# Adding two product pairs of a seven-product block in PSUM, with one product of each block issued behind the first of the next

## What is computed

```
def hybrid_mixer(xn, ...):
    z = xn @ w_in                                   # 7 x 1024 columns: u, v, b_gate, c_gate, x_in, r_a, r_b
    u, v = gelu(u), layer_norm(gelu(v))
    y_a = (u * chunk_spatial_mix(v, w_s, b_s)) @ w_a_out
    y_b = (b_gate * short_conv(c_gate * x_in)) @ w_b_out
    return (sigmoid(r_a) * y_a + sigmoid(r_b) * y_b) @ w_o

x = x + rms_norm(hybrid_mixer(rms_norm(x)))
x = x + rms_norm((silu(xf @ w_gate) * (xf @ w_up)) @ w_down)      # xf = rms_norm(x), hidden width 2816
```

## Time and profile before

| | us |
|---|---|
| three timed runs | 1603.54, 1603.16, 1603.20 |
| their median | 1603.2 |
| span of the profiled execution | 1601.0 |
| TensorE busy | 1590.6 (99%) |
| VectorE busy | 1081.9 (68%) |
| ScalarE busy | 559.8 (35%) |
| GpSimd busy | 703.9 (44%) |

### The profile page before, as it was taken

How to read it: one execution, slowest core, us unless ns; L and a number is a source line. 1 busy time by engine, 2 the same in 40 slices (tenths; PEclk the granted TensorE clock), 3 DMA queues, 4 the chain that set the end, 5 groups by cost and what they waited for, 6 DMA issues and landing times.

```text
span 1601.0 us, 30253 instructions
## 1 busy us (share of the span) xinstructions
PE 1590.6 (99%) x12427; PEld 1542.2 (96%) x12427; DVE 1081.9 (68%) x1463; ACT 559.8 (35%) x852; POOL 703.9 (44%) x512
## 2 busy tenths in 40 slices
PE   9999999999999999999999999999999999999998
PEld 6889999999999999999978999999999999999997
DVE  8757857797793338868965666766666666575766
ACT  4222332222223336333434532333332233352544
POOL 1011534544544444644730324544444443545375
PEclk9999999999999999999999999999999999999999
DMA  6202011431423333474423313533333345472723
GB/s 216 79 1 80 27 54 34 126 96 44 126 82 110 109 106 121 149 242 133 148 91 120 131 41 110 155 105 100 106 104 104 105 124 178 153 239 80 238 107 133
DMA packets 155283, 184.38 MB, mean 115 GB/s; under 512 B 7355, under 2 KB 138035, under 8 KB 155147
## 3 DMA queue, kind: packets, MB, share of 16 engines
q1 hardware_dynamic: 154987, 182.41, 35.7%
q10 hardware_dynamic: 160, 0.04, 0.0%
HBM read 133.74 MB, written 48.72 MB: 114 GB/s over the span
## 4 chain that ended last, share of the span: by engine, by line
PE 95%; DVE 1%; DMA 1%; POOL 1%; issue 1%; SPq 0%; ACT 0%; DVEq 0%; ACTq 0%; POOLq 0%
PE ps L414 91%; PE ps L449 1%; PE ps L526 1%; DMA pre_gain<-in_mix_pre_g 1%; DVE tp L2213 1%; PE ps L669 0%; PE ps L653 0%; PE ps L424 0%; DMA tp_f<-hid_dram 0%; SPq L783 0%; DVE s_bc L2232 0%; POOL ring_lo L1108 0%; POOL ring_lo L1095 0%; PE ps L503 0%; DVE g L2234 0%
## 5 line engine op out<-in xcount | busy, mean ns | idle before, releaser
L414 PE MATMUL ps<-tp,ring_hi 128*128 128x258 f32 x7292 | 1182.9, 283 | 0.5 <-issue 0.3
L414 PEld LDWEIGHTS ps<-tp,ring_hi 128*128 128x128 f32 x7292 | 1010.6, 190 | 0.9 <-issue 0.5
L414 PE MATMUL ps<-tp,ring_lo 128*128 128x258 f32 x3646 | 744.8, 283 | 0.0
L414 PEld LDWEIGHTS ps<-tp,ring_lo 128*128 128x128 f32 x3646 | 571.3, 190 | 0.0
L1095 POOL TENSOR_TENSOR ring_lo<-ring_f,ring_hi 128x512 fp32r<-128x512 f32 (+1 forms) x228 | 328.3, 1460 | 365.1 <-DVE ring_f L1840 212.5
L1095 POOL TENSOR_TENSOR ring_lo<-stage,ring_hi 128x512 fp32r<-128x512 f32 (+1 forms) x199 | 304.7, 1540 | 400.3 <-ACT ring_hi L1240 399.6
L1240 ACT ACTIVATE ring_hi<-ring_f 128x512 fp32r<-128x512 f32 (+1 forms) x228 | 142.6, 627 | 519.9 <-DVE ring_f L1835 196.2
L1240 ACT ACTIVATE ring_hi<-stage 128x512 fp32r<-128x512 f32 (+1 forms) x199 | 122.0, 617 | 121.1 <-PE ps L414 63.5
L1832 DVE TENSOR_TENSOR ring_f<-stage 128x512 f32<-128x512 f32 (+1 forms) x57 | 46.8, 821 | 135.2 <-PE ps L414 82.7
L1853 DVE TENSOR_TENSOR s_a<-ps,s_a 128x516 f32<-128x516 f32 (+1 forms) x58 | 39.8, 686 | 51.9 <-PE ps L414 51.4
L414 PE MATMUL ps<-tp 128*128 128x512 f32 (+1 forms) x384 | 72.0, 340 | 0.0
(11 more groups left out here) (243 smaller groups left out, 1453.9 us busy)
## 6 DMA issues: line engine op xcount, KB each, us to landing
stage<-in_w_in SPq DMA_DIRECT2D x24, 1024.0 KB, 5.9
ht_dram<-ht SPq DMA_DIRECT2D x44, 258.0 KB, 4.2
hid_dram<-hq SPq DMA_DIRECT2D x40, 258.0 KB, 3.1
stage<-in_w_gate SPq DMA_DIRECT2D x10, 1024.0 KB, 6.6
stage<-in_w_up SPq DMA_DIRECT2D x10, 1024.0 KB, 5.3
tp_f<-hid_dram SPq DMA_DIRECT2D x16, 516.0 KB, 5.5
tp_f<-ht_dram SPq DMA_DIRECT2D x16, 516.0 KB, 8.7
stage<-in_w_down SPq DMA_DIRECT2D x8, 1024.0 KB, 7.1
```

What stands on the lines that cost most here:

```text
L414: ins = pe.matmul(o, w, xc, start=first and n == 0, stop=last and n == 2)
```

## The change

- `PBANK` is another one: products 0 and 2 both land in Y, 4 and 6 both in X. Products 2 and 6 don't clear their pair, so Y then holds P0 + P2, and X holds P4 + P6.
- c11 = P0 + P2 is not made by DVE any more: its consumer reads it in PSUM (`c11_act` on ACT; a product or `gather` on DVE). u1 and u2 become one operation, `u2` = P3 + s1; `u4` = P1 + u2; c22 = P4 + u4, c12 = P5 + u4, c21 = (P4 + P6) + u2. DVE has two operations fewer in each of the 58 runs. Seven runs whose c11 had been put straight to its place have an ACT copy for it.
- The waits of TensorE are now: product 2 for s1 (P0 must be copied before P2 is added to it), 5 for u2, 6 for c22, all of the same run; of the run before, product 0 waits for the reader of c11 (Y), 1 for u4 (W), 3 for c12 (Z), 4 for c21 (X). The first half of a plain run (Z) waits for c12.
- Where a run and its next both have seven products (`piped`), the order is 1, 2, 3, 4, 5 of r, then 0 of r+1, then 6 of r, then 1 of r+1. Before plain runs and at run 2 it is not so.
- The buffers `s_a` and `s_b` take turns as the place of s1 and u2, so s1 of a run doesn't wait for c21 of the run before.

```diff
-PBANK = [Z, W, Y, X, Z, Y, X]
+PBANK = [Y, W, Y, Z, X, Z, X]
...
+def piped(run):
+    return 2 < run < len(RUNS) - 1 and RUNS[run][0] not in QORDER and RUNS[run + 1][0] not in QORDER
+ORDER = []
+for r, (b, _) in enumerate(RUNS):
+    seq = [(r, i) for i in range(1 if piped(r - 1) else 0, 4 if b in QORDER else 7)]
+    if piped(r):
+        seq.insert(-1, (r + 1, 0))
+    ORDER += seq
...
-                    pe.wait_ge({Z: u2_done, W: c22_done, Y: c12_done, X: c21_done}[pair], SIDX[r])
+                    pe.wait_ge(*(c11_read(r) if pair == Y else ({W: u4_done, Z: c12_done, X: c21_done}[pair], SIDX[r])))
             def product(r, p):
+                if p == 6 and piped(r):
+                    issue(r + 1, 0)
+                if p or not piped(r - 1):
+                    issue(r, p)
+            def issue(r, p):
                 pe.wait_ge(w_lo, lo_at(b, p))
-                if p == 4:
+                if p == 2:
                     pe.wait_ge(s1_done, SIDX[r])
                 elif p == 5:
-                    pe.wait_ge(c11_done, SIDX[r])
+                    pe.wait_ge(u2_done, SIDX[r])
                 elif p == 6:
-                    pe.wait_ge(u1_done, SIDX[r])
+                    pe.wait_ge(c22_done, SIDX[r])
...
-                                kp == 0, kp == kps(b) - 1)
+                                kp == 0 and p not in (2, 6), kp == kps(b) - 1, p in (2, 6))
...
             def s1(r):
                 act.wait_ge(prod_done, done(r, 0))
-                if SIDX[r] > 1:
-                    act.wait_ge(c21_done, SIDX[r] - 1)
-                act.activation(s_a[:, gs], reg(Z, gs), ACT.Copy).then_inc(s1_done, 1)
+                if RUNS[r - 1][0] not in QORDER and taken(r - 1, 2):
+                    act.wait_ge(*taken(r - 1, 2))
+                if RUNS[r - 2][0] not in QORDER:
+                    act.wait_ge(*(taken(r - 2, 4) or (c21_done, SIDX[r - 2])))
+                act.activation(s_turn[r % 2][:, gs], reg(Y, gs), ACT.Copy).then_inc(s1_done, 1)
...
+            def c11_act(r, dst, func):
+                act.wait_ge(prod_done, done(r, 2))
+                return act.activation(dst, reg(Y, RUNS[r][1]), func)
...
+            def u2(r):
+                dve.wait_ge(prod_done, done(r, 3))
+                dve.wait_ge(s1_done, SIDX[r])
+                dve.tensor_tensor(s_turn[r % 2][:, gs], reg(Z, gs), s_turn[r % 2][:, gs], ADD).then_inc(u2_done, 1)
+            def u4(r, dst):
+                dve.wait_ge(u2_done, SIDX[r])
+                dve.tensor_tensor(dst, reg(W, gs), s_turn[r % 2][:, gs], ADD).then_inc(u4_done, 1)
+            def c22(r, dst, mid):
+                dve.wait_ge(prod_done, done(r, 4))
+                dve.tensor_tensor(dst, reg(X, gs), mid, ADD).then_inc(c22_done, 1)
```

More of the change, by code:

```diff
@@ L71 @@
 LOADS = [STAGE[:b + 1].count(STAGE[b]) for b in range(B_END)]
+def piped(run):
[6 more added lines that the diff above has]
+    ORDER += seq
+DONE = {at: n + 1 for n, at in enumerate(ORDER)}
 def done(run, i):
-    return BASE[run] + i + 1
+    return DONE[run, i]
 def used(b, pos):
@@ L409, in _, with three @@
         def _(pe):
-            def three(outs, w_h, w_l, x_h, x_l, first, last):
+            def three(outs, w_h, w_l, x_h, x_l, first, last, onto=False):
                 ins = None
@@ L413, in three @@
                     for o, xc in zip(outs, x):
-                        ins = pe.matmul(o, w, xc, start=first and n == 0, stop=last and n == 2)
+                        ins = pe.matmul(o, w, xc, start=first and n == 0, stop=last and n == 2, skip_group_check=onto)
                 return ins
@@ L1327, in _ @@
                 s1(r)
-                prepare(r + 1)
+                mp, kind = divmod(r - B_C, 3)
+                if kind == 0:
+                    prepare(r + 1, 0, 3)
+                    if mp:
+                        act.wait_ge(ht_ready, 4 * mp)
+                        act.wait_ge(q_saved[0], 16 * mp)
+                    else:
+                        act.wait_ge(u_prod, 4 * MP)
+                    c11_act(r, q[:, 0], ACT.Copy).then_inc(c11_copied, 1)
+                    prepare(r + 1, 3)
+                else:
+                    prepare(r + 1)
             def a_split(n):
@@ L1600, in _ @@
                 prepare(b + 1, 0, 2)
-                silu(0, c11_done, r)
+                if j == 1:
+                    act.wait_ge(hid_saved[0], 16)
+                else:
+                    act.wait_ge(hid_ready, 4 * (j - 2) + 1)
+                c11_act(r, q[:, 0], ACT.Silu).then_inc(silu_ready, 1)
                 prepare(b + 1, 2, 5)
@@ L1671, in _ @@
                     s1(r)
-                    prepare(b + 1)
+                    if kb == 0:
+                        prepare(b + 1, 0, 3)
+                        for n in range(4):
+                            act.wait_ge(hid_saved[n], 16 * J)
+                            act.wait_ge(ht_saved[n], 16 * (MP + J))
+                        c11_down(r)
+                        prepare(b + 1, 3)
+                    else:
+                        prepare(b + 1)
                     if mp == MP - 2:
@@ L1975, in c_run @@
                         dve.wait_ge(q_saved[n], 16 * mp)
-                c11(r, q[:, 0])
                 middle(r, r + 1, q[:, 1])
-                c22(r, q[:, 3])
+                c22(r, q[:, 3], q[:, 1])
                 sums(r + 1, 2)
@@ L2126, in _ @@
                     at_total(1)
-                u2(r)
-                if last:
                     a_rest(2)
-                c22(r, q[:, 3])
+                c22(r, q[:, 3], q[:, 1])
                 sums(r + 1, 2)
@@ L2504, in down_rest @@
                     y_root_of(0)
-                u2(r)
-                dve.wait_ge(ready, count + 1)
-                c22(r, s_b[:, gs])
+                c22(r, s_turn[(r + 1) % 2][:, gs], s_c[:, gs])
                 sums(nb, 2)
@@ L2549, in _ @@
                     t_rest(1, 5)
-                c11(r, g[:, m, 0])
-                u1(r)
-                u3(r, g[:, m, 1])
+                u2(r)
+                u4(r, g[:, m, 1])
                 sums(b + 1, 1)
```

242 lines of the change are left out of this document (128 added, 114 removed).

## The result

The changed kernel takes 1631.5 us (median of 4 runs, 1630.7 to 1632.2), the kernel before 1603.4 in the same session: a ratio of 1.0174, with an interval of 1.0159 to 1.0188. It is 28 us slower, where these executions of one kernel lie within 1.6 us of each other. The profiled execution has a span of 1629.2 us against 1601.0.

What follows compares the result with a forecast made beforehand. The prediction took TensorE's stream without holes as the bound. Its terms, mostly waits at stage borders plus a clock fall, summed to 22.9 us, taking the median from 1603.2 to 1626.1 us; the range was 1610 to 1636.

Steps and rivals of the forecast that it cites:

- run 27: At a border, product 6 waits for c22, which stands behind `b_rest` on DVE: 0.5 us (0 to 0.7).
- TensorE's stream is the time: Whole kernel: TensorE runs without holes, busy 1590.6 of 1601.0 us; DVE's 80 us count only where they help a deadline.
- Steady runs cost nothing: Away from stage borders, some 45 of the 58 runs meet the new deadlines: cost 0, with 0.7 us to spare.
- Rival 3: A wait in each steady run: about 36 runs stop 0.5 us each on s1, +18, so 1644; chance 0.10.
- rivals 1 and 2: The first: all waits are covered, 1602 to 1604, chance 0.07; the second: DVE's relief removes interior holes, 1601.8, chance 0.03.
- Run 23: At a border, 1.2 us on s1 behind `a_split` and 5.3 on c22 behind `a_rest`: together 6.5 (3.5 to 6.8).
- Runs 29, 59, 63, 67, 68: Product 2 waits for s1 behind splits, roundings, squares or a table load: 1.6, 1.1, 0.4, 2.35 and 2.7 us.
- Run 66: Near the end, s1 stands behind the square and scaling of what c21 brought: 0.9 us.
- Run 57: After a plain run, product 0 lands in Y and waits for the third copy of the run before: 1.3 us.
- Runs 60 and 64: First halves of these plain runs wait for c12: 2.7 less 0.9 of present holes in the former, 1.9 in the latter.
- The clock: Half rate on TensorE after the 5.3 us stop on c22: 2.1 us (0 to 2.5), no other fall counted.
- Rival 4: Borders cost half, as queues before c22 and c12 shrink, and the clock doesn't fall: 1612 to 1618; chance 0.20.

Runs made afterwards that it cites:

- run 22: Not a follow-up: one of the kernel's own numbered runs of products; its product 6 ended at 607.6 us in the kernel before.
- The mended kernel: The changed kernel with only places of instructions in the ACT, DVE and SyncE queues changed, at the borders where it stops: 1606.5 us over 11 runs, ratio 1.0015.
- the first experiment: The changed kernel with product 0 of the next run never issued ahead of product 6, all else kept: 1635.1 us, ratio 1.0199.
- run 26: Not a follow-up: one of the kernel's own numbered runs of products; the change issues its product 6 one slot later, with c21 behind it.
- The experiment with the transfer: The changed kernel with the load for block 28's operand moved in SyncE's queue ahead of the load that waits for c21: 1626.7 us, ratio 1.0138.

## Why the prediction was right, and where it was off

The sign, the size and all places but one were right: 1626.1 predicted, 1610 to 1636 the range, 1631.5 measured. Three things in it were wrong: run 27, the list of clock falls, and the reading of c22 in the runs with a convolution, which cost nothing by luck. Point by point:

- **The reading that TensorE's stream is the time**, and that DVE's 80 us are worth nothing: right. DVE lost 99 us, and TensorE got nothing for it.
- **Steady runs cost nothing**: right, 0.2 us idle in 610, and up to run 22 TensorE's stream isn't later than before. The mended kernel shows it again, since with the borders mended 25 of 28 us go. But the reason given ("c22 0.7 after product 4, as DVE is idle there") holds only in some of them. In runs 6, 9, 12 and 15 c22 comes 5.3 us after, and 0.3 us were left of the 5.62. The prediction hadn't looked there; without the cover of product 0 these four runs stop, as the first experiment shows. Rival 3, a wait in each steady run, is refuted by the same windows; rivals 1 and 2 by the result.
- **Run 23** (6.5): 6.3, right in both its parts. The end of c22 was 0.2 us off, with two errors of 1.1 us that cancel (above).
- **Runs 29, 59, 63, 67, 68** on s1: all within 0.25 us. Run 66 was 0.6 short. The 3.64 us of run 67 have an s1 of 0.37 in them; with one of 0.58 they are 3.85, not 3.65, and the addition before the square took 1.47 us here, 1.24 in the row of run 67 that it was priced by.
- **Run 57** 1.3, was 0.75; another profile of a variant had 1.8 in the same place. The copy follows a transfer, and the bounds of 0.6 to 2.0 are what one sees.
- **Run 27** (0.5): wrong, 2.79. The step that failed is "c22 stands behind `b_rest`, which ended 708.50". I took this end as fixed and shifted nothing, though I had written that everything behind product 6's result comes a slot later. `b_rest` hangs on a split, this on a transfer, and the transfer on SyncE's queue behind c21 of run 26. The experiment with the transfer shows it: moved past that wait, the stop is gone. It was a queue that I didn't follow.
- **Runs 60 and 64**: 1.8 and 1.9 predicted, 1.4 and 1.0 measured. Ahead of run 60 the trace has two stops, as c22 is late before c12 is; the prediction named only c12. Ahead of c22 a `t_rest` took 2.95 us instead of 2.30. Ahead of run 64 it is the other way, 2.29 instead of 3.10, and that is 0.8 of the 0.9 by which the term was too large.
- **The clock**: the term of 2.1 behind run 23 was near (2.4), its list too short. I gave it to a stop of 5 us alone; the clock fell behind 2.27 and 2.50 us as well (1.5 + 1.6). With run 27's 2.3 and the 0.3 behind run 23 this is 5.7 us. The prediction was short by 5.3 (by spans), as the other terms together came out a little low.
- The rule of the Trainium skill, page "TensorE: Matmul & The Clock Gate", section "Why this matters for your kernels", that gaps between bursts of matmuls put TensorE back to half rate, holds here (the clock fell behind all 9 stops of 3.15 us and more), and for shorter stops than the one for which I had used it (15 of 20 of 2.0 to 2.83 us).

Rival 4 (1612 to 1618, the borders cost half) is refuted by the result, and its reason was wrong: c22 of run 23 came 0.9 us later than before, not sooner, and the clock did fall behind it.

The cause of the slowdown, then, as far as the runs show it: the change makes c22, c12 and s1 due sooner, and product 6 with all that is queued behind it one slot later; that costs at the borders, where the queues of DVE, ACT and SyncE hold preparations ahead of them. Changing only places in these queues gives back 25 of 28 us.

## What to carry to other kernels

When TensorE has no holes, a lighter DVE is worth nothing, and a change to banks and waits is a change of deadlines: write for each wait how many slots lie between, and compare with how late the operation ends in every run, not in a typical one (here one steady run had 4.9 us to spare on c22, another 0.3). Follow a moved product through every queue that its result releases, SyncE's included, before a neighbour is called fixed. A cover that one half of a change provides (here product 0 ahead of product 6) must be priced with it taken away, in the runs where the queue is longest.

## What the runs showed of the hardware

The granted clock fell more readily than I expected. In the interior of the profiles of the ten kernels other than the one before, none of 35 stops of 1.0 to 1.94 us was followed by a fall to 0.50, 15 of 20 of 2.0 to 2.83 were, and all 9 of 3.15 to 5.5. The same stop of the same kernel line went either way: 2.79 and 2.75 us in run 27 without one, 2.83 and 2.79 with one. A fall cost 1.5 to 1.6 us behind stops of up to 3.5 us, and 2.0 to 2.7 behind those of 4.0 and more, on top of the stop.

A second thing: operations of DVE that write little (128x16) took 0.16 us in most rows and 1.26 in some, and pairs of large ones 2.3 or 3.4 us. Such rows were in the trace of before too, and they move c22 and c12 by up to 1.1 us. The traces show what the long ones share. In that of before, 155 operations of DVE lasted at least 0.5 us longer than the quickest quarter of their kind (operation and shape, from PSUM or not). All 155 overlapped an operation of POOL and were still at work when it ended. The row of 1.26 us at 628.24 ends with this one:

```profile
628.01 1.46 POOL L1095 TENSOR_TENSOR ring_lo<-stage,ring_hi 128x512 fp32r<-128x512 f32 x1 [2.60 <-ACT ring_hi L1240]
```

None of the 155 reads PSUM, and 245 operations that do read it overlapped POOL and kept their usual time. In the changed kernel it is 133 of 133, and none from PSUM. An overlap isn't enough: of the 1229 at their usual time 391 had one. So the long rows go with POOL's work, and a forecast of a deadline on DVE should look at POOL's queue too. No run here moved an operation of POOL to prove it.
